# Three score banks two steps ahead in the attention, and two banks in turn for its dense chunks

## What is computed

```python
for l in range(DEPTH):                                   # 2 layers
    h = rmsnorm(x, norm_mix_g[l])
    proj = einsum('bsd,dn->bsn', h, w_in[l])             # one wide projection, split into:
    (c_q, c_kv, k_r, q_b, k_b, v_b, f_logit, conv_in, gate_logit) = split(proj)
    o_a = block_attention(qa, ka, va, mla_scale, chunk_mask)          # 8 heads, latent attention
    o_b = block_attention(qf, kf, vf, fox_scale, frame_mask, cum)     # 8 heads, from q_b, k_b, v_b
    u = silu(layernorm(causal_depthwise_conv(glu(conv_in))))          # 31 taps, 512 channels
    y = g_a * (o_a @ w_bo_a) + g_b * (o_b @ w_bo_b) + g_c * (u @ w_bo_c)
    x = x + y @ w_out[l]
    x = x + (silu(h2 @ w_ffn_gate[l]) * (h2 @ w_ffn_up[l])) @ w_ffn_down[l]

def block_attention(q, k, v, scale, diag_mask, cum=None):   # blocks of 128 queries
    for q0 in range(0, 512, 128):
        s = q[q0:q0+128] @ k[:q0+128].T * scale              # 128, 256, 384 or 512 keys
        p = softmax(where(mask, s, -inf)); outs.append(p @ v[:q0+128])
```

## Time and profile before

| | before |
|---|---|
| median of 3 runs | 1798.65 us (1798.49 to 1798.70) |
| the profiled execution | 1799.9 us |
| its span in the trace | 1798.1 us |
| mean granted TensorE clock | 0.995 |
| TensorE busy | 1740.6 us, 97% of the span |
| VectorE busy | 1088.5 us, 61% |
| ScalarE busy | 673.0 us, 37% |
| attention of the first layer, 137.6 to 336.0 us | TensorE busy 188.4, VectorE 153.5, ScalarE 86.3 |

### The profile page before, as it was taken

How to read it: one execution, slowest core, us unless ns; L and a number is a source line. 1 busy time by engine, 2 the same in 40 slices (tenths; PEclk the granted TensorE clock), 3 DMA queues, 4 the chain that set the end, 5 groups by cost and what they waited for, 6 DMA issues and landing times.

```text
span 1798.1 us, 21975 instructions
## 1 busy us (share of the span) xinstructions
PE 1740.6 (97%) x7813; PEld 1374.8 (76%) x7813; DVE 1088.5 (61%) x1647; ACT 673.0 (37%) x1125; POOL 205.2 (11%) x145
## 2 busy tenths in 40 slices
PE   5999999999999999999999999999999999999998
PEld 4777666777888888888877766678778888888886
DVE  7688778767555555543348878768665555555322
ACT  4454444434343232222235544444343432322222
POOL 3620100010020000001125201000100200000010
PEclk9999999999999999999999999999999999999999
DMA  4432111233333333333333321113333333333331
GB/s 123 103 79 68 48 48 48 65 89 94 94 106 95 103 94 93 98 91 97 94 85 73 95 55 48 47 36 98 86 91 112 94 96 103 94 93 95 92 97 67
DMA packets 308468, 152.19 MB, mean 85 GB/s; under 512 B 30436, under 2 KB 307166, under 8 KB 308396
## 3 DMA queue, kind: packets, MB, share of 16 engines
q1 hardware_dynamic: 308096, 151.05, 30.2%
q10 hardware_dynamic: 300, 0.19, 0.0%
HBM read 149.09 MB, written 2.10 MB: 84 GB/s over the span
## 4 chain that ended last, share of the span: by engine, by line
PE 83%; DVE 11%; ACT 3%; issue 2%; DMA 0%; ACTq 0%; SPq 0%; DVEq 0%
PE bank L1284 64%; PE bank L1360 10%; PE bank L1341 3%; PE bank L1393 2%; DVE w_lo L904 2%; PE bank L1372 2%; ACT w_hi L615 1%; DVE c_acc L964 1%; DVE q_t L991 1%; DVE h_lo L933 1%; DVE k_t L994 0%; DVE tmp L925 0%; DVE p_b L976 0%; PE bank L1309 0%; DVE c_raw L1113 0%
## 5 line engine op out<-in xcount | busy, mean ns | idle before, releaser
L615 ACT CAST w_hi<-raw 128x1024 fp32r<-128x1024 f32 (+4 forms) x330 | 301.4, 916 | 732.9 <-PE bank L1284 732.2
L904 DVE TENSOR_TENSOR w_lo<-raw,w_hi 128x1024 fp32r<-128x1024 f32 (+4 forms) x330 | 356.3, 1083 | 249.7 <-ACT w_hi L615 247.9
L1284 PE MATMUL bank<-h_hi,w_hi 128*128 128x512 f32 (+1 forms) x1200 | 474.8, 396 | 10.4 <-DVE w_lo L904 5.4
L1284 PE MATMUL bank<-h_hi,w_lo 128*128 128x512 f32 (+1 forms) x1200 | 468.1, 390 | 0.0
L1284 PE MATMUL bank<-h_lo,w_hi 128*128 128x512 f32 (+1 forms) x1200 | 468.0, 390 | 0.0
L1284 PEld LDWEIGHTS bank<-h_hi,w_hi 128*128 128x128 f32 (+1 forms) x1200 | 225.0, 187 | 69.7 <-issue 12.2
L1284 PEld LDWEIGHTS bank<-h_lo,w_hi 128*128 128x128 f32 (+1 forms) x1200 | 225.2, 188 | 48.8 <-issue 2.5
L1284 PEld LDWEIGHTS bank<-h_hi,w_lo 128*128 128x128 f32 (+1 forms) x1200 | 225.1, 188 | 48.4
L925 DVE TENSOR_TENSOR tmp<-bank,rstd_x 128x512 f32<-128x512 f32 x140 | 96.7, 690 | 264.0 <-PE bank L1284 259.1
L964 DVE SCALAR_TENSOR_TENSOR c_acc<-u_pad,dwk_l,c_acc 128x512 f32<-128x512 f32 x240 | 173.9, 746 | 1.1
L504 POOL TENSOR_TENSOR x_acc<-x_acc,x_sq 128x512 f32<-128x512 f32 x39 | 66.8, 1712 | 881.7 <-ACT x_sq L625 549.0
(11 more groups left out here) (207 smaller groups left out, 2154.6 us busy)
## 6 DMA issues: line engine op xcount, KB each, us to landing
raw<-in_w_in SPq DMA_DIRECT2D x96, 512.0 KB, 3.8
raw<-in_w_ffn_gate SPq DMA_DIRECT2D x44, 512.0 KB, 3.7
raw<-in_w_ffn_up SPq DMA_DIRECT2D x44, 512.0 KB, 3.8
raw<-in_w_ffn_down SPq DMA_DIRECT2D x32, 512.0 KB, 3.7
raw<-in_w_out SPq DMA_DIRECT2D x16, 512.0 KB, 3.8
raw<-in_w_ffn_down SPq DMA_DIRECT2D x16, 384.0 KB, 3.4
raw<-in_w_bo_a SPq DMA_DIRECT2D x16, 256.0 KB, 2.7
raw<-in_w_bo_b SPq DMA_DIRECT2D x16, 256.0 KB, 2.7
```

The costliest lines, as they stand in the source:

```text
L615: last = nc.scalar.copy(to, of)
L904: last = nc.vector.tensor_tensor(to, of, part.bitcast(F32), ALU.subtract)
L1284: ins = nc.tensor.matmul(bank_t[0:rows, :], wt[slot][:, w], x, start=first and k == 0 and p == 0, stop=last and k == k_tiles - 1 and p == 2)
```

## The change

- There are three score banks instead of four (`SCORE_BANKS`), the bank of step g being (g+2) mod 3 (`score_slot`). TensorE makes the scores of step g+2 in step g, not of g+3, and only those of steps 0 and 1 before the 64 steps. The scores of step g wait for the exponential of step g-3.
- The freed fourth bank and `stat_bank` take the dense chunks in turn (`feed_bank`). The first unit of chunk n waits for the evacuation of chunk n-2.
- VectorE evacuates a chunk that ended in step e in its step e+2, behind `normalise(e+1)`, and no longer in step e+1.
- After the attention, the first chunks of the merge wait for the exponentials of three banks and not four.

```diff
+SCORE_BANKS = 3
-RAW_CREDIT, EVAC_CREDIT, EXP_CREDIT, ... = RAW, BANKS, BANKS, 2, 1, 1
+RAW_CREDIT, EVAC_CREDIT, EXP_CREDIT, ... = RAW, BANKS, SCORE_BANKS, 2, 1, 1
+def score_slot(g):
+    return (g + 2) % SCORE_BANKS
+        feed_bank = (stat_bank, s_bank[SCORE_BANKS])
...
     # VectorE, attention
+                    from_bank = feed_bank[FEED.index(name) % 2]
...
-                    nc.vector.tensor_reduce(neg_max[:, q:q + 1], s_bank[q][:, 0:(q + 1) * P], AX_X, ALU.max,
+                    nc.vector.tensor_reduce(neg_max[:, q:q + 1], s_bank[score_slot(g)][:, 0:(q + 1) * P], AX_X, ALU.max,
...
-                    if g - 1 in FEED_END:
-                        put(FEED[FEED_END.index(g - 1)])
+                    if g - 2 in FEED_END:
+                        put(FEED[FEED_END.index(g - 2)])
...
     # TensorE, attention
-                    bank_t = stat_bank if n < len(FEED) else s_bank[0]
+                    bank_t = feed_bank[n % 2] if n < len(FEED) else s_bank[0]
...
-                        pe.wait_ge(evac_done, fed + min(n, len(FEED) - 1))
+                        pe.wait_ge(evac_done, fed + max(n - 1, 0))
...
                 logits(1)
-                logits(2)
                 for g in range(STEPS):
-                    if g + 3 < STEPS:
-                        logits(g + 3)
+                    if g + 2 < STEPS:
+                        logits(g + 2)
...
-                    if m < BANKS:
+                    if m < SCORE_BANKS:
                         pe.wait_ge(exp_done, ex.value + 1 + m)
```

More of the change, by code:

```diff
@@ L80 @@
 DOWN_K = (8, 8, 6)
-RAW_CREDIT, EVAC_CREDIT, EXP_CREDIT, TURN_CREDIT, O_CREDIT, STD_CREDIT = RAW, BANKS, BANKS, 2, 1, 1
+RAW_CREDIT, EVAC_CREDIT, EXP_CREDIT, TURN_CREDIT, O_CREDIT, STD_CREDIT = RAW, BANKS, SCORE_BANKS, 2, 1, 1
 CONV_TAPS = (0, 0, 1, 1, 2, 2, 3, 3)
@@ L658, in attention @@
                     w = (s % 4 + 1) * P
-                    nc.scalar.activation(p_b[:, P_AT[s % 4]:P_AT[s % 4] + w], s_bank[s % 4][:, 0:w], ACT.Exp,
+                    nc.scalar.activation(p_b[:, P_AT[s % 4]:P_AT[s % 4] + w], s_bank[score_slot(g)][:, 0:w], ACT.Exp,
                                          bias=neg_max[:, s % 4:s % 4 + 1],
@@ L980, in put @@
                     kind, pair = name[0], int(name[1])
+                    from_bank = feed_bank[FEED.index(name) % 2]
                     if kind == "g":
-                        evacuated(nc.vector.tensor_tensor(q_t[:, pair, :], stat_bank[:], rstd_x[:], ALU.mult))
+                        evacuated(nc.vector.tensor_tensor(q_t[:, pair, :], from_bank[:], rstd_x[:], ALU.mult))
                     elif kind == "v":
@@ L985, in put @@
                             dve.wait_ge(vt_done, vt.value + (pair - 1))
-                        evacuated(nc.vector.tensor_tensor(tmp[pair % 2][:], stat_bank[:], rstd_x[:], ALU.mult))
+                        evacuated(nc.vector.tensor_tensor(tmp[pair % 2][:], from_bank[:], rstd_x[:], ALU.mult))
                     else:
@@ L990, in put @@
                             if kind == "q":
-                                ins = nc.vector.scalar_tensor_tensor(q_t[0:NOPE, 2 * pair + e, :], stat_bank[rows, :], FOX_SCALE,
+                                ins = nc.vector.scalar_tensor_tensor(q_t[0:NOPE, 2 * pair + e, :], from_bank[rows, :], FOX_SCALE,
                                                                      rstd_x[rows, :], ALU.mult, ALU.mult)
                             else:
-                                ins = nc.vector.tensor_tensor(k_t[0:NOPE, 2 * pair + e, :], stat_bank[rows, :], rstd_x[rows, :], ALU.mult)
+                                ins = nc.vector.tensor_tensor(k_t[0:NOPE, 2 * pair + e, :], from_bank[rows, :], rstd_x[rows, :], ALU.mult)
                         evacuated(ins)
@@ L1339, in logits @@
                     w = (q + 1) * P
-                    ins = nc.tensor.matmul(s_bank[q][:, 0:w], q_t[0:rows, head, q * P:w], k_t[0:rows, head, 0:w], start=True, stop=True)
+                    b = s_bank[score_slot(g)]
+                    ins = nc.tensor.matmul(b[:, 0:w], q_t[0:rows, head, q * P:w], k_t[0:rows, head, 0:w], start=True, stop=True)
                     if kind == 1:
-                        ins = nc.tensor.matmul(s_bank[q][:, q * P:w], ident_b[:], mask_b[:], start=False, stop=True, skip_group_check=True)
+                        ins = nc.tensor.matmul(b[:, q * P:w], ident_b[:], mask_b[:], start=False, stop=True, skip_group_check=True)
                     ins.then_inc(score_done, 1)
```

## The result

| | before | after |
|---|---|---|
| median | 1798.68 us (4 runs, 1798.49 to 1798.84) | 1780.89 us (4 runs, 1780.69 to 1782.45) |
| ratio | | 0.9901, 95% interval 0.9890 to 0.9913 |
| profiled execution | 1799.9 us, span 1798.1 | 1782.45 us, span 1780.6 |
| first attention, first score to the first matmul of the merge | 136.8 to 335.8 us, 198.9 | 137.0 to 326.4 us, 189.4 |
| second attention, the same | 1015.3 to 1212.6 us, 197.3 | 1005.9 to 1195.1 us, 189.2 |

The kernel got 17.8 us faster, 1.0%, where 18.9 was forecast; the time, 1780.89, lies 1.1 us above the forecast and inside the range.

What follows compares the result with a forecast made beforehand. TensorE, busy 97% of the span, bounds the kernel, so only its stops count. Gain 20.6 - 1.7 = 18.9 us takes the profiled 1799.9 to 1781.0; the median, 1.25 lower, is 1779.8 us, range 1774 to 1787.

Steps and rivals of the forecast that it cites:

- the term of 20.6 us: Both attentions: losses of the ten chunk steps and their wakes go, 10.33 us in the first layer, 10.27 in the second.
- TensorE's stop there is gone, whatever VectorE does: A chunk's first unit: with the second dense bank it needs only the evacuation of the chunk before the last.
- The stops that stay: Steps 19 and 43 still wait, 1.9 to 2.2 us, for an untouched chain behind the values; step 1 stays too.
- the term of 1.7: Steps 19 and 43, both layers: narrower scores leave 0.42 us less covered work in four places, 1.7 us lost.
- Two steps ahead: Maxima could wait for scores made one step later: taken as 0, bounds 0 to 0.4 us for each of 14 values.
- The room: Transposes of steps 9 to 17, the tightest stretch: VectorE's part 21.3 us, TensorE's 21.6; a lag of single tenths can stay.
- The clock: Low clock after step 43, first layer, costing 1.36 us in step 44: may not return, worth 0 to 1.4, taken as 0.
- Half of it: Rival: waits at the transposes stay, 4.0 us a layer; gain 10.9 us, time 1788 us; chance 0.14.
- Slower: Rival: moved evacuations make transposes two steps on late by their whole length, 36.0 us in all; 1815.8 us; chance 0.03.
- More falls of the clock: Rival: the low clock comes in each pair of heads, 14 times 1.4 us; time 1799 us; chance 0.03.
- Nothing happens: Rival: the stop is only moved, VectorE's evacuation still being what the next unit needs; chance 0.04.
- The weight loads' rows: Alternative sum from idle time before TensorE's weight loads, 12.1 us a layer: 22.5 us gain in place of 18.9; not used.

Runs made afterwards that it cites:

- the early evacuation: The kernel after with VectorE evacuating a dense chunk one step after its end, as before, the two banks in turn kept: 1798.99 us, ratio 1.0000 to before.
- the scores alone: The kernel after with one bank for the dense chunks and the early evacuation, leaving three score banks and scores two steps ahead: 1799.27 us.
- after, rounding first: The kernel after with ScalarE's weight rounding put ahead of the copies behind the values in steps 18 and 42: 1770.88 us, ratio 0.9843 to before.
- the doubled evacuations: The kernel after with the earlier rounding, VectorE doing every evacuation of a dense chunk in the attention twice: 1785.75 us, ratio 0.9925 to before.
- late evacuation: The kernel before with only the evacuation moved one step later, one dense bank and scores three steps ahead: 1798.51 us, ratio 0.9996.

## Why the prediction was right

**The reading.** TensorE and VectorE wait for each other around a chunk's end, and both stops go together: right. The ten chunk steps and their wakes (7, 14, 17, 21, 25, 28, 29, 31, 38, 41, 45, 55) lose nothing in the kernel after, in either layer; the term of 20.6 us holds. Step 17 was to take 2.4 us and took 2.36. No waits for the normalisation came up in steps 8, 11, 12 or 25.

**One sentence of it was wrong.** "TensorE's stop there is gone, whatever VectorE does" is true of the wait and not of the time: with the early evacuation the kernel is no faster. The prediction priced the stop at the unit and the late normalisation as two amounts; they were two loops through the same instruction, of which only the longer counted. The sum came out right because the change cuts both.

**The stops that stay**, 19 and 43, were to take 1.9 to 2.2 us and took 1.94, 2.13, 1.94 and 1.94. Their growth by 0.42 us is what was measured (1.52 to 1.94). That this chain is ScalarE's rounding behind the copies is shown by taking it away: 7.95 us back. As an amount for the scores alone the term of 1.7 was too large; that kernel lost 0.7.

**Two steps ahead**: taken as 0, and the kernel after shows no late transpose for want of scores. The prediction named more than 1 us of VectorE's waits at the maximum as a sign of being wrong. They came to 9.0 us in the first attention, and it was the sign that was wrong: VectorE waited there because it was ahead, and with the rounding first it waits for 9.4 us at the maximum while the whole attention loses 0.25. The room is not without end: one step costs 25 us.

**A slip in the room.** The prediction gives TensorE 21.6 us between the transposes of steps 9 and 17. By its own lengths it is 18 units, the transposes and scores of eight steps, the values and one value transpose: 12.4 + 6.5 + 2.5 + 0.45 = 21.9. This makes VectorE's room there larger and changes nothing in the sum.

**The clock** is the likeliest place of the 1.1 us. I took its fall as unchanged or gone; in the profiled execution there were two, 3.3 us, where there had been one of 1.4. A second fall was among the prediction's signs of being wrong, and it is why the second attention is 8.1 us shorter and not 9 to 10. The reason given for hoping it would go was misread too: step 42 of the kernel before has no stop. The stops in front of the fall were those of 41 and 43; 41 went, and the clock fell behind 43 all the same. Profiled to profiled the gain is 1799.9 - 1782.45 = 17.45, and 18.9 less the 1.95 us more of slow clock is 16.95, which leaves 0.5. The timed runs of both kernels lie in a band of about the width of one such fall (1798.3 to 1800.3 before, over all its runs; 1780.7 to 1782.45 after), and "after, rounding first" varies by 0.08 us. By this reading the median run before had no fall and the median run after one, and 18.9 + 0.5 - 1.65 is the 17.8 measured. It is a reading and not shown: only profiled executions show the clock stretch by stretch, the kernels with two banks and early evacuation and with the scores alone vary by 4.2 and 5.2 us, and the five other kernels in whose profiles no such fall appears vary by 0.25 to 1.24.

**The rivals.** "Half of it" (VectorE keeps the transposes late): it did not happen. "Slower": the doubled evacuations show the mechanism exists and that 18 us of work a layer is then paid for by 7; with single evacuations the room of 2 us is enough. "More falls of the clock" happened once, not in each pair of heads. "Nothing happens" did not come, but either half of the change alone brings just that.

**The weight loads' rows** would have given 22.5 us. The distances between starts gave 18.9, nearer to the 17.8 measured.

## What to carry to other kernels

When two engines exchange a buffer once in a while inside a list that they also walk step by step, look for every loop through the exchange: a second buffer opens one, and moving the emptying behind the next step's urgent work opens the other; either alone brought nothing in sum here, and both together 18 us. Before adding up idle rows, take the stretch between two starts of the same instruction and compare it with an undisturbed one; this told the gain to a few us, the idle rows did not. And in an engine with several duties in a step, do first what another engine waits for and last what itself waits: one such exchange of two lines on ScalarE brought 8 of the last 10 us.

## What the runs showed of the hardware

In the attentions the granted clock of TensorE fell to 0.50, its lower level of 1.2 GHz, for 3.4 us in some executions, each time right behind a stop of step 19 or 43 that cost 1.7 us or more: step 44 before, steps 44 and 20 after, 44 with the early evacuation, 20 with the scores alone. It cost 1.36 to 1.67 us each time. Behind equally long stops in the same programs it did not fall (1.94 us in step 19 of the first layer after), and in the six kernels whose stops are shorter or of 1.5 to 1.7 us (late evacuation, and all with the rounding first) none was seen in the attentions. A stop of 2 us can thus cost 3.6 (1.94 + 1.64). Near the start of the program the low clock cost nothing that can be seen: between 17 and 31 us from the start the clock stood at 0.50 for 3.4 to 10.2 us in nine of the ten profiled executions and in the kernel after not at all, and the first attention begins between 136.6 and 137.2 us in all of them.
